# The level products of a chunkless HGRN2 recurrence: later query columns only, and one masked copy a level

## The reference

```
o_t  = q_t exp(b_t) S + sum over s <= t of A[t, s] v_s
A[t, s] = sum over e of q[t, e] * exp(b[t, e] - b[s, e]) * k[s, e]       (b: running sum of the log forget gates)
S_new = exp(b_last) S + sum over s of k_s exp(b_last - b_s) v_s^T
```

## Time and profile before

| | us |
|---|---|
| Median of 3 runs (lowest, highest) | 2584.43 (2578.24, 2594.58) |
| The profiled execution's own time | 2585.26 |
| Its span (first to last instruction) | 2583.5 |
| PE busy in the span | 2315.0 |
| DVE busy | 1100.4 |
| ScalarE busy | 708.8 |

### The profile page before, as it was taken

One profiled execution on the slowest core, in us unless ns is written; L12 is line 12 of the kernel. 1 busy time (PEld: TensorE's weight loads), 2 busy tenths in 40 slices (PEclk: granted clock), 3 DMA queues, 4 the chain that ended last, 5 costly groups with the idle time before them and its releaser, 6 DMA issues. The chain is left out here.

```text
span 2583.5 us, 36454 instructions
## 1 busy us (share of the span) xinstructions
PE 2315.0 (90%) x15002; PEld 1669.0 (65%) x15002; DVE 1100.4 (43%) x1673; ACT 708.8 (27%) x900; POOL 33.0 (1%) x30
## 2 busy tenths in 40 slices
PE   6966768899898888999998799998999999998998
PEld 4645756443333333333332699987999999978998
DVE  4646433212111111221111565666655655666654
ACT  3332111111010000010100443534433433535332
POOL 0002100000000000000000000000000000000000
PEclk8957877899999999999999799999999999999999
DMA  9630022699999999999998555532555555423561
GB/s 372 232 148 1 1 66 78 267 415 416 418 416 417 417 417 416 416 417 417 417 417 356 159 194 182 163 112 82 180 180 186 172 183 188 152 91 107 179 195 66
DMA packets 235967, 627.04 MB, mean 243 GB/s; under 512 B 13084, under 2 KB 153916, under 8 KB 199772
## 3 DMA queue, kind: packets, MB, share of 16 engines
q1 hardware_dynamic: 232796, 622.68, 64.2%
q10 hardware_dynamic: 3072, 2.93, 0.4%
HBM read 624.53 MB, written 1.05 MB: 242 GB/s over the span
## 5 line engine op out<-in xcount | busy, mean ns | idle before, releaser
L1535 PE MATMUL bank<-ring,xt 128*64 128x512 f32 x2048 | 472.5, 601 | 53.9 <-DMA ring<-in_exp_w_dram 51.9
L1799 DVE TENSOR_TENSOR w_low<-ring,w_high 128x2048 fp32r<-128x2048 f32 x168 | 383.9, 2290 | 308.0 <-ACT w_high L1794 307.7
L1794 ACT ACTIVATE w_high<-ring 128x2048 fp32r<-128x2048 f32 x168 | 320.0, 1909 | 276.1 <-PE bank L1989 138.2
L1535 PEld LDWEIGHTS bank<-ring,xt 128*64 128x64 f32 x2048 | 134.7, 137 | 375.4 <-issue 216.6
L1561 PE MATMUL bank<-ring,ut 128*64 128x512 f32 x1024 | 236.2, 599 | 35.6 <-DMA ring<-in_exp_w_dram 34.2
L2004 PE MATMUL bank<-h_high,w_high 128*128 128x256 f32 x1408 | 186.5, 281 | 14.3 <-ACT h_high L1889 14.3
L1561 PEld LDWEIGHTS bank<-ring,ut 128*64 128x64 f32 x1024 | 67.0, 136 | 191.7 <-issue 105.7
L1619 ACT ACTIVATE sg<-glu 128x512 f32<-128x512 f32 x32 | 20.2, 631 | 612.1 <-DVE glu L1682 612.1
L2004 PE MATMUL bank<-h_low,w_high 128*128 128x256 f32 x1408 | 185.4, 280 | 0.0
L2004 PE MATMUL bank<-h_high,w_low 128*128 128x256 f32 x1408 | 185.3, 280 | 0.0
L2004 PEld LDWEIGHTS bank<-h_high,w_high 128*128 128x128 f32 x1408 | 175.2, 188 | 15.1 <-ACT h_high L1889 14.9
(11 more groups left out here) (509 smaller groups left out, 2875.5 us busy)
## 6 DMA issues: line engine op xcount, KB each, us to landing
ring<-in_exp_w_dram SPq DMA_DIRECT2D x384, 1024.0 KB, 22.4
ring<-in_ffn_w_gate_dram SPq DMA_DIRECT2D x44, 1024.0 KB, 5.4
ring<-in_ffn_w_up_dram SPq DMA_DIRECT2D x44, 1024.0 KB, 5.4
ring<-in_ffn_w_down_dram SPq DMA_DIRECT2D x44, 1024.0 KB, 4.9
ring<-in_w_in_dram SPq DMA_DIRECT2D x36, 1024.0 KB, 5.4
ring<-in_ada_w_dram SPq DMA_DIRECT2D x24, 1024.0 KB, 12.9
ring<-in_w_out_dram SPq DMA_DIRECT2D x8, 1024.0 KB, 5.2
ring<-in_w_o_dram SPq DMA_DIRECT2D x4, 1024.0 KB, 8.9
```

Of the source, the lines that this page charges most:

```text
L1535: ins = nc.tensor.matmul(bank[b][at:at + SLOTS, :], xt[:, c, SLOTS * side:SLOTS * side + SLOTS], ring[:, c, 512 * q:512 * q + 512], start= ...
L1794: nc.scalar.activation(w_bufs[0][u % BUFS], ring2[:, u % RING2, :], ACT.Copy).then_inc(high2, 1)
L1799: nc.vector.tensor_tensor(w_bufs[1][u % BUFS], ring2[:, u % RING2, :], w_bufs[0][u % BUFS].bitcast(F32), ALU.subtract).then_inc(low2, 1)
```

## The change

For levels 1 to 7 PE multiplies only the query columns of the later halves: every block's second b of 2b columns, 64 of 128, so that all 8 products of a level fill one bank of 512 columns, bank 7 for odd levels and bank 6 for even ones. Level 0 is as before. The masks keep 64 columns for levels 1 to 7. One masked copy a level takes [8 products, blocks, b] from the bank into columns that lie evenly spaced; for that, `at_` now covers all of `hT` with four blocks a head (the fourth unused), so that the eight diagonal blocks lie at a stride of 256 columns (`on_diagonal`). Level 0 takes two copies instead of four. The waits are counted anew: `level(n)` on PE waits for the copy of level n - 2 (both copies of level 0 for n = 1 and 2), `cross` for that of level 6.

```diff
-        levels.append((i[:, None] // (2 * b) == i[None] // (2 * b)) & (i[None] % (2 * b) >= b) & (i[:, None] % (2 * b) < b))
+        later = i[i % (2 * b) >= b]
+        levels.append((i[:, None] // (2 * b) == later[None] // (2 * b)) & (i[:, None] % (2 * b) < b))
...
+LEVEL_COLS = P + (NLEV - 1) * P // 2
...
-        level_masks = sb("level_masks", [P, NLEV, P], U8)
+        level_masks = sb("level_masks", [P, LEVEL_COLS], U8)
...
-        at_ = hT[:, 2:8, :].rearrange("p c t -> p (c t)").rearrange("p (h b t) -> p h b t", h=4, b=3)
+        at_ = hT[:, :, :].rearrange("p c t -> p (c t)").rearrange("p (h b t) -> p h b t", h=4, b=4)
+        on_diagonal = hT[:, :, :].rearrange("p c (two t) -> p c two t", two=2)[:, :, 0, :]
...
-                nc.gpsimd.memset(at_[:, :, :, :], 0.0).then_inc(sem(f + "cleared"), 1)
+                nc.gpsimd.memset(on_diagonal, 0.0).then_inc(sem(f + "cleared"), 1)
...
-                    for h in range(4):
-                        if n and h % 2 == 0:
-                            pe.wait_ge(sem(f + "masked_in"), 2 * (n - 1) + h // 2 + 1)
-                        for a in range(TT):
-                            at = P * (2 * (h % 2) + a)
-                            ins = nc.tensor.matmul(bk[6 + h // 2][:, at:at + P], kr[:, h, P * a:P * a + P], qp[:, h, P * a:P * a + P],
-                                                   start=True, stop=True)
-                        if h % 2:
-                            ins.then_inc(sem(f + "level_ready"), 1)
+                    if n == 0:
...
+                    else:
+                        pe.wait_ge(sem(f + "masked_in"), max(2, n))
+                        for h in range(4):
+                            for a in range(TT):
+                                at = P // 2 * (2 * h + a)
+                                later = qp[:, h, P * a:P * a + P].rearrange("p (k two b) -> p k two b", two=2, b=2 ** (n - 1))[:, :, 1, :]
+                                ins = nc.tensor.matmul(bk[6 + n % 2][:, at:at + P // 2], kr[:, h, P * a:P * a + P], later, start=True, stop=True)
+                        ins.then_inc(sem(f + "level_ready"), 1)
...
                     pe.wait_ge(sem(f + "factors"), NLEV)
-                    pe.wait_ge(sem(f + "masked_in"), 2 * NLEV)
+                    pe.wait_ge(sem(f + "masked_in"), NLEV)
...
-                    dve.wait_ge(sem(f + "level_ready"), 2 * n + 2)
+                    dve.wait_ge(sem(f + "level_ready"), n + 2)
...
-                    for j in range(2):
-                        blocks = at_[:, 2 * j:2 * j + 2, :, :].rearrange("p h b t -> p (h b) t")
-                        for h in range(2):
-                            ins = nc.vector.copy_predicated(blocks[:, 3 * h:3 * h + 3:2, :], level_masks[:, n:n + 1, :].to_broadcast([P, 2, P]),
-                                                            bk[6 + j][:, T * h:T * h + T].rearrange("p (a t) -> p a t", a=2))
-                        st.tell(ins, f + "masked_in")
+                    if n == 0:
+                        for j in range(2):
+                            st.tell(nc.vector.copy_predicated(on_diagonal[:, 4 * j:4 * j + 4, :], level_masks[:, 0:P].unsqueeze(1).to_broadcast([P, 4, P]),
+                                                              bk[6 + j][:, :].rearrange("p (c t) -> p c t", c=4)), f + "masked_in")
+                    else:
+                        b = 2 ** (n - 1)
+                        at = P + P // 2 * (n - 1)
+                        mask = level_masks[:, at:at + P // 2].rearrange("p (k b) -> p k b", b=b).unsqueeze(1).to_broadcast([P, DC, P // (2 * b), b])
+                        later = on_diagonal.rearrange("p c (k two b) -> p c k two b", two=2, b=b)[:, :, :, 1, :]
+                        st.tell(nc.vector.copy_predicated(later, mask, bk[6 + n % 2][:, :].rearrange("p (c k b) -> p c k b", c=DC, b=b)), f + "masked_in")
```

More of the change, by code:

```diff
@@ L1738, in build @@
         prods = sb("prods", [P, 4 * T])
-        levels = prods[:, 0:NLEV * P]
+        levels = prods[:, 0:LEVEL_COLS]
         rope2 = sb("rope2", [P, 2, T])
@@ L2234, in level @@
                         pe.wait_ge(sem(f + "factors"), n)
-                    for h in range(4):
-                        if n and h % 2 == 0:
-                            pe.wait_ge(sem(f + "masked_in"), 2 * (n - 1) + h // 2 + 1)
-                        for a in range(TT):
-                            at = P * (2 * (h % 2) + a)
-                            ins = nc.tensor.matmul(bk[6 + h // 2][:, at:at + P], kr[:, h, P * a:P * a + P], qp[:, h, P * a:P * a + P],
-                                                   start=True, stop=True)
-                        if h % 2:
-                            ins.then_inc(sem(f + "level_ready"), 1)
+                    if n == 0:
+                        for h in range(4):
+                            for a in range(TT):
+                                at = P * (2 * (h % 2) + a)
+                                ins = nc.tensor.matmul(bk[6 + h // 2][:, at:at + P], kr[:, h, P * a:P * a + P], qp[:, h, P * a:P * a + P],
+                                                       start=True, stop=True)
+                            if h % 2:
+                                ins.then_inc(sem(f + "level_ready"), 1)
+                    else:
+                        pe.wait_ge(sem(f + "masked_in"), max(2, n))
+                        for h in range(4):
+                            for a in range(TT):
+                                at = P // 2 * (2 * h + a)
+                                later = qp[:, h, P * a:P * a + P].rearrange("p (k two b) -> p k two b", two=2, b=2 ** (n - 1))[:, :, 1, :]
+                                ins = nc.tensor.matmul(bk[6 + n % 2][:, at:at + P // 2], kr[:, h, P * a:P * a + P], later, start=True, stop=True)
+                        ins.then_inc(sem(f + "level_ready"), 1)
                 def cross():
                     pe.wait_ge(sem(f + "factors"), NLEV)
-                    pe.wait_ge(sem(f + "masked_in"), 2 * NLEV)
+                    pe.wait_ge(sem(f + "masked_in"), NLEV)
                     for h in range(4):
@@ L2521, in level @@
                         st.step(nc.vector.tensor_tensor(k4[:, :, 0, :], k4[:, :, 0, :], halves[:, :, 1:2].to_broadcast([P, blocks, b]), ALU.mult), f + "factors")
-                    for j in range(2):
-                        blocks = at_[:, 2 * j:2 * j + 2, :, :].rearrange("p h b t -> p (h b) t")
-                        for h in range(2):
-                            ins = nc.vector.copy_predicated(blocks[:, 3 * h:3 * h + 3:2, :], level_masks[:, n:n + 1, :].to_broadcast([P, 2, P]),
-                                                            bk[6 + j][:, T * h:T * h + T].rearrange("p (a t) -> p a t", a=2))
-                        st.tell(ins, f + "masked_in")
+                    if n == 0:
[8 more added lines that the diff above has]
+                        st.tell(nc.vector.copy_predicated(later, mask, bk[6 + n % 2][:, :].rearrange("p (c k b) -> p c k b", c=DC, b=b)), f + "masked_in")
                 def take_cross():
-                    dve.wait_ge(sem(f + "level_ready"), 2 * NLEV + 1)
-                    dve.wait_ge(sem(f + "masked_in"), 2 * NLEV)
+                    dve.wait_ge(sem(f + "level_ready"), NLEV + 2)
+                    dve.wait_ge(sem(f + "masked_in"), NLEV + 1)
                     st.tell(nc.vector.tensor_copy(at_[:, :, 1, :], bk[6][:, :].rearrange("p (h t) -> p h t", h=4)), f + "at_ready")
@@ L2625, in vector @@
                 posf, angle, turns = masked[:, 0, 0, :], masked[:, 0, 1, :], masked[:, 1, 0, :]
-                nc.vector.tensor_copy(flat(level_masks[:, :, :]), levels)
+                nc.vector.tensor_copy(level_masks[:, :], levels)
                 st.step(nc.vector.tensor_copy(posf, posi2[:, :]))
```

## The result

The changed kernel took 2598.38 us (median of 5 runs, 2595.53 to 2604.02) against 2584.43 of the kernel before (5 runs, 2576.40 to 2594.58): ratio 1.0063, 95% interval 1.0039 to 1.0087. It is 14 us slower, by less than 1%, and outside the range given. The profiled execution of the changed kernel is the one of 2598.38 us, span 2596.7.

What follows compares the result with a forecast made beforehand. PE, 90% busy, was taken as the bound. Per layer +0.3 (half columns), +0.53 (level 1), -0.74 (L2225) and -0.74 (cross product), times two layers, gave -1.3 us: 2583 us, range 2570 to 2594.

Steps and rivals of the forecast that it cites:

- part 3, "small ones": Smaller clearing of diagonal blocks, mask cast and masks' load: 0 each (-0.3 us if the cast's cover were gone).
- Half the columns on PE: Level matmuls, levels 1 to 7: 64 columns no quicker than 128, 107 to 112 ns an instruction, +0.3 us a layer.
- The rival by which columns set the pace: Level instructions fall from 107 to 54 ns, 11.9 us less in all, giving 2571 us; chance 0.07.
- Operand with holes: Gapped moving operand in levels 1 and 2: taken as nothing, at most 1.7 us a layer (+3.4, 2586.5); chance 0.06.
- One copy a level: DVE's masked copies: 0.60 us instead of 1.34, saving 0.74 each in levels 1 to 7, 5.3 us a layer, mostly idle time.
- sign of being wrong: Masked copies on DVE taking over 1 us each, where about 0.7 us was expected.
- The waits that were to go: PE's waits before L2225, 1.05 us to about 0.3 (-0.74), and before the cross product, 1.23 us to under 0.3.
- gain of 0.74 us at the cross product: PE's 1.23 us wait there goes nearly whole; 0.74 us a layer kept, 0.5 moves to the wait at 1779.12.
- Level 1: PE waits for both of level 0's copies, not the first pair: wait 1.64 to about 2.2 us, +0.53 a layer.
- The wait ahead of the turning behind unit 13: PE's wait at 1779.12, 1.25 us before: grows to at least 1.7, up to 3.4 with cross product and unit 13 at full clock.
- The rival: Granted clock falls before level 1 in both layers, about 1.6 us a fall: +1.9 us, 2586; chance 0.2.
- a second place for the same fall: Clock also falls at the longer wait before 1779.12: another 1.6 us a layer, 2589 or 2590; within the 0.2 rival.

Runs made afterwards that it cites:

- kernel before at the new addresses: Kernel before with a 576-byte filler in the mask tile's place and the mask tile at the end, so later buffers lie as in the changed kernel: 2593.28 us, ratio 1.0043.
- padded changed kernel: Changed kernel with the mask tile kept at its old 1024 bytes a partition, so later buffers keep their old addresses: 2588.78 us, ratio 1.0031.
- half-column kernel: Kernel before, but levels 1 to 7 multiply only the first 64 query columns of each product; copies, waits, addresses untouched: 2583.41 us, ratio 1.0001.
- three padded changed kernels: Changed kernel with old-size mask tile: as is 2588.78 us; level banks swapped 2587.64; cross product again waiting for level 7's copy 2587.11.
- two filled kernels: Changed kernel at old addresses, banks swapped, useless matmuls in PE's wait behind unit 13: 2582.59 us, ratio 1.0012; also before level 1: 2584.61 us, 0.9999.

## Why the prediction was wrong

The forecast was -1.3 us (2583); measured +14 (2598.38), outside of 2570 to 2594.

- **The failed step** is in part 3, "small ones": "The masks' load shrinks alike, once, a whole feed-forward stage ahead of use: 0", and the same for the cast. The smaller tile was priced by the instructions that touch it, and not by what it moves. It shifted the moving operands of some 8000 matmuls by 448 bytes against their weights: 10 to 12 us at equal clock, shown by the kernel before at the new addresses (+10 on the line, ratio 1.0043) and by the padded changed kernel, whose pace came back. The range was bounded by the priced edits and knew nothing of this.
- **Half the columns on PE** was right: 1.70 us a level, 106 ns an instruction where 107 to 112 was given, and the half-column kernel at 1.0001. The rival by which columns set the pace is refuted here, for matmuls that each load 128 columns of weights. The price of +0.3 us a layer was not there (0.0). The Trainium skill ("TensorE: Matmul & The Clock Gate", section "Back-to-back issue gap") gives the formula by moving columns for the isolated matmul only and says that in a stream of weight loads and matmuls both set the spacing. So it was a stretch of the formula when the prediction took a halved slot from it for its rival. The 106 ns, unchanged with half the columns, fit what the page says of streams.
- **Operand with holes** (levels 1 and 2): the levels at 1691.45 and 1701.52 take 1.78 and 1.70 us to the next start, the first as long as before (1.78): no cost.
- **One copy a level** was half right: 0.7 us from level 3 on, but 1.3 at levels 1 and 2, where over 1 us had been named as a sign of being wrong. These two feed no wait of PE. The waits that were to go went: the values' matmul waits for nothing, the cross product neither. But the gain of 0.74 us at the cross product was not kept, since the wait behind unit 13 grew by 2.1 us.
- **Level 1** waits 1.97 us, +0.33 where +0.53 was worked out (2.2 in the padded kernel, as given).
- **The wait ahead of the turning behind unit 13** was given as at least 1.7, up to 3.4 if the clock doesn't fall at the cross product; it measured 3.35. In the kernel before at the new addresses, where the clock did not fall at the cross product, it is 2.79; so the 1.25 that the prediction started from was the wait of a PE slowed by the fall. The rival named it as "a second place for the same fall" at 1.6 us a layer, and there the clock fell (0.52); at its first place, level 1, it did not in this profile, though it did in the padded kernel's (0.57 over the 4 us behind its level 1). The rival had the right mechanism with 0.2 of chance, and 2589 or 2590 with both places, 5 us above the kernel before; the three padded changed kernels lost 8 to 10 (0.5 to 15 by their intervals).
- So the sum of the parts that it did price, at the old addresses, came out at +8 us and not -1.3: the waits saved were there, and what they left behind, one long wait, cost more in clock than they gave. In the forecast's sum the clock stood at nothing; it had its place in a rival only. That rests on the 40 stages and on the two filled kernels, and is less firm than the price of the addresses.
- That the rival's 2589 or 2590 stands so close to the padded kernel's 2588.78 is partly luck: it counts a fall at level 1 in both layers, and the padded kernel's profile has it in one.

## What to carry to other kernels

A change of a tile's size moves every tile allocated behind it; where PE streams from those tiles back to back, compare the pace of untouched matmuls (their count in a window of full busy time) before explaining anything by the edit, and pad the tile to compare like with like. Work that is narrower but has the same number of weight loads gives PE nothing. A wait that is removed and comes back as one longer wait can cost more than it gave, because the granted clock may fall behind it. Before pricing a saved wait, look at whether the clock had fallen there: the next wait may be short only because of that.

## What the runs showed of the hardware

- float32r matmuls of 256 columns, each with its own 128x128 weight load, ran at 113.3 to 120.0 ns from start to start at full granted clock, depending on the distance of weights and moving operand in SBUF; moving both by 128 bytes left 117.8. At some distances (64, 128 and 192 modulo 256 among them) two paces occur, each held for tens of us or more.
- A masked copy of 512 float32 elements from PSUM took 0.69 to 0.74 us with destination runs of 4 to 64 elements, and 1.30 to 1.32 us with runs of 2 and 1. A tensor_tensor with every second element took 0.69.
- float32 matmuls with 128x128 weights took 106 to 107 ns an instruction for 64 as for 128 moving columns (111 in level 1 with either).
- The kernel before varied from 2569.28 to 2593.35 us over its 105 later runs, and most of that goes with the mean granted clock of the run, 1.3 us per 0.001.
- The granted clock fell to half behind a wait of 3.3 us or more in 10 stages of 10, and behind waits of 2.7 to 3.0 us at the same place in 6 of 13.
